# Delta rule: both passes prepared in slots of the gate chunks

## What is computed

```python
r, kr, vr, z_b, w_down, a_down = _split(_token_shift(u_rwkv, mu), RWKV_SIZES)
w = -jax.nn.softplus(-(rwkv_w0 + jnp.tanh(w_down) @ rwkv_w2)) - 0.5
decay = jnp.exp(-jnp.exp(w))                  # exp(-exp(-0.5) * sigmoid(...))
a = jax.nn.sigmoid(rwkv_a0 + a_down @ rwkv_a2)
kk = heads(kr * rwkv_k_k); kk = kk / jnp.maximum(norm(kk), L2_EPS)
kr = kr * (1.0 + (a - 1.0) * rwkv_k_a)
def step(S, inp):                             # over the tokens, the delta rule
    sa = jnp.einsum('bhvk,bhk->bhv', S, -kk_t)
    S = S * w_t + sa * (kk * a)_t + v_t * k_t
    return S, jnp.einsum('bhvk,bhk->bhv', S, r_t)
y = groupnorm(y) * rwkv_ln_w + rwkv_ln_b
bonus = jnp.sum(r * kr * rwkv_r_k, -1) * vr
o_b = (y + bonus) * jax.nn.silu(z_b)
m = sigmoid(g_a) * (o_a @ w_proj_fox) + sigmoid(g_b) * (o_b @ w_proj_rwkv)
return x + m @ w_out
```

## Time and profile before

| | us |
|---|---|
| runs | median 3121.57 of 3 (3117.95 to 3123.22) |
| profiled execution | 3119.44, its span 3117.5 |
| TensorE busy | 2993.9 (96%) |
| DVE busy | 1848.9 (59%) |
| ACT busy | 1371.2 (44%) |
| mean granted clock of TensorE | 0.977 of full |

### The profile page before, as it was taken

The page is one execution under the profiler, slowest core; times in us unless marked ns, Lnnn a source line. Parts: engine busy times, 40 slices in busy tenths (PEclk is TensorE's granted clock), DMA queues, the critical chain, the costliest instruction groups (busy, mean ns, idle before and its releaser), DMA issues.

```text
span 3117.5 us, 45946 instructions
## 1 busy us (share of the span) xinstructions
PE 2993.9 (96%) x17935; PEld 2484.0 (80%) x17935; DVE 1848.9 (59%) x2047; ACT 1371.2 (44%) x1876; POOL 344.8 (11%) x371
## 2 busy tenths in 40 slices
PE   8999999999999987999999999999999999986898
PEld 6888788788888877888888888887888888765786
DVE  5555567856665769455555555556445664467664
ACT  5555454343444454444444344445444444422244
POOL 2000011930001948000000000000000000000000
PEclk9999999999999987999999999999999999988999
DMA  7555476675757984566566665655666678701364
GB/s 242 173 171 165 153 223 200 218 224 168 223 186 240 244 255 120 170 193 211 186 193 189 190 188 189 190 185 168 179 198 192 189 213 255 215 23 46 121 211 155
DMA packets 302691, 580.98 MB, mean 186 GB/s; under 512 B 21512, under 2 KB 40200, under 8 KB 300832
## 3 DMA queue, kind: packets, MB, share of 16 engines
q1 hardware_dynamic: 285696, 522.85, 54.5%
q0 software_dynamic: 9264, 37.29, 4.2%
q10 hardware_dynamic: 7536, 18.06, 1.9%
HBM read 550.35 MB, written 21.50 MB: 183 GB/s over the span
## 4 chain that ended last, share of the span: by engine, by line
PE 90%; DVE 6%; ACT 1%; issue 1%; POOL 1%; DMA 1%; ACTq 0%; SPq 0%; DVEq 0%; POOLq 0%
PE acc L940 26%; PE acc L947 26%; PE acc L941 26%; PE tp L955 2%; DVE wL L2260 2%; PE acc L1568 1%; PE acc L1569 1%; PE acc L1575 1%; PE tp L1481 1%; PE acc L1479 1%; PE wk L1226 0%; POOL xs L883 0%; DVE A L3049 0%; PE acc L1241 0%; DMA raw<-in_a_w_in_dram 0%
## 5 line engine op out<-in xcount | busy, mean ns | idle before, releaser
L2260 DVE TENSOR_TENSOR wL<-raw,wH 128x1024 fp32r<-128x1024 f32 (+1 forms) x968 | 1227.4, 1276 | 1124.8 <-ACT wH L1603 1122.9
L1603 ACT CAST wH<-raw 128x1024 fp32r<-128x1024 f32 (+1 forms) x968 | 1009.6, 1045 | 1416.2 <-PE acc L947 1227.2
L940 PE MATMUL acc<-wH,xH 128*128 128x512 f32 (+1 forms) x2208 | 866.5, 393 | 7.0 <-DVE xL L2314 4.2
L941 PE MATMUL acc<-wH,xL 128*128 128x512 f32 (+1 forms) x2208 | 856.8, 389 | 0.0
L940 PE MATMUL acc<-wH,hH 128*128 128x512 f32 x1536 | 603.5, 393 | 1.9 <-DVE hL L2314 1.9
L941 PE MATMUL acc<-wH,hL 128*128 128x512 f32 x1536 | 600.0, 391 | 0.0
L947 PE MATMUL acc<-wL,xH 128*128 128x512 f32 (+1 forms) x2208 | 588.1, 388 | 1.2 <-DVE wL L2260 1.2
L940 PEld LDWEIGHTS acc<-wH,xH 128*128 128x128 f32 x2208 | 415.9, 188 | 94.9 <-issue 5.0
L947 PEld LDWEIGHTS acc<-wL,xH 128*128 128x128 f32 x2208 | 413.1, 188 | 87.5 <-DVE wL L2260 1.9
L941 PEld LDWEIGHTS acc<-wH,xL 128*128 128x128 f32 x2208 | 416.1, 188 | 82.8
L947 PE MATMUL acc<-wL,hH 128*128 128x512 f32 x1536 | 412.4, 390 | 5.8 <-DVE wL L2260 5.7
(11 more groups left out here) (461 smaller groups left out, 2195.3 us busy)
## 6 DMA issues: line engine op xcount, KB each, us to landing
raw<-in_mlp_w_dram SPq DMA_DIRECT2D x512, 512.0 KB, 3.8
raw<-in_w_in_dram SPq DMA_DIRECT2D x192, 512.0 KB, 3.8
raw<-in_a_w_in_dram SPq DMA_DIRECT2D x96, 512.0 KB, 3.8
raw<-in_b_w_glu_dram SPq DMA_DIRECT2D x64, 512.0 KB, 3.6
raw<-in_a_w_out_dram SPq DMA_DIRECT2D x32, 512.0 KB, 3.7
raw<-in_w_out_dram SPq DMA_DIRECT2D x32, 512.0 KB, 4.5
raw<-in_w_proj_fox_dram SPq DMA_DIRECT2D x16, 512.0 KB, 4.8
raw<-in_w_proj_rwkv_dram SPq DMA_DIRECT2D x16, 512.0 KB, 4.4
```

What stands on the lines that cost most here:

```text
L940: nc.tensor.matmul(bank, aH[:, k, rows], wH[:, j % SPLIT, u, 0:n], start=k == 0, stop=False)
L941: nc.tensor.matmul(bank, aL[:, k, rows], wH[:, j % SPLIT, u, 0:n], start=False, stop=False)
L1603: nc.scalar.copy(wH[:, j % SPLIT, :, 0:n], raw[:, j % RAW, :, 0:n]).then_inc(high_done, 1)
L2260: nc.vector.tensor_tensor(wL[:, j % SPLIT, :, 0:n], raw[:, j % RAW, :, 0:n], wH[:, j % SPLIT, :, 0:n].bitcast(F32), ALU.subtract).then_inc ...
```

## The change

Both passes are prepared inside the slots of the gate chunks. For that each pass has its own buffers, only four banks are used (C[0] to C[3], once the attention's), and the steps are laid out over ten slots per pass: p = 3 + 10 m + s. TensorE makes `lin` at s = 0, `cum` at s = 2, the totals at s = 4, transposes at s = 6 and s = 8. The biases come as a row of weights against a row of ones. The three triangles of the sums become two: they hold ones and are fp32r, the sigmoid is split into a rounded part and a rest (`sgH`, `sgL`), the inclusive sum is the exclusive one plus the sigmoid itself (on DVE), and the factor goes into the scale of the exponential. The vectors are loaded by POOL, three of them one after the other through one buffer, `par`.

On POOL, while the constants are made and after the token shift's loads:

```diff
+    for e, by in enumerate((1, -1)):
+        blocks(decay[:, e], 1.0)
+        keep(decay[:, e], [[by, P]], -1, -by)
...
+    pool.wait_ge(f_dve, FDVE["og", 1])
+    for m in range(MT):
+        for v, (low, bias) in enumerate((("rwkv_w2_2", "rwkv_w0_2"), ("rwkv_a2_2", "rwkv_a0_2"))):
+            pool.dma_start(lw2[m][0:LORA, v], I[low][0]).then_inc(r_low_in[m], 16)
+            pool.dma_start(lw2[m][LORA:LORA + 1, v], I[bias]).then_inc(r_low_in[m], 16)
+        if m == 0:
+            pool.wait_ge(shift_out, 17)
+            bcast("rwkv_k_k_2", par[:], r_par_in)
+    for m in range(MT):
+        if m:
+            pool.wait_ge(r_dve, RDVE["kt", m - 1])
+            bcast("rwkv_k_k_2", par[:], r_par_in)
+        pool.wait_ge(r_dve, RDVE["kk0", m])
+        bcast("rwkv_k_a_2", par[:], r_par_in)
+        pool.wait_ge(r_dve, RDVE["ka", m])
+        pool.dma_start(par[:], I["rwkv_r_k_2"].rearrange("o h n -> o (h n)").broadcast_to([P, H1])).then_inc(r_par_in, 16)
+    pool.wait_ge(r_pe, RPE["L", 0])
+    bcast("rwkv_ln_w_2", lnw[:], r_ln_in)
+    bcast("rwkv_ln_b_2", lnb[:], r_ln_in)
```

On TensorE, the steps (in `prep_lin`, `prep_cum`, `prep_tot`, `prep_turn`), the slots and what waits there:

```diff
+    for v in range(2):
+        for q in range(2):
+            last = nc.tensor.matmul(C[2 * v + q], lT[:, v, m * P:m * P + P], lw2[m][:, v, q * NW:(q + 1) * NW],
+                                    start=True, stop=True)
+    RPE.mark(r_pe, last, "lin", m)
...
+    wait(name_dve=("sgL", m))
+    wait(("siga", m))
+    for e in range(2):
+        for q in range(2):
+            bank = C[2 * e + q]
+            cols = slice(q * NW, (q + 1) * NW)
+            nc.tensor.matmul(bank, decayR[:, e], sgH[m][:, cols], start=True, stop=False)
+            last = nc.tensor.matmul(bank, decayR[:, e], sgL[m][:, cols], start=False, stop=True)
+    RPE.mark(r_pe, last, "cum", m)
...
+    wait(("E3", m))
+    for p in range(R_PAIRS):
...
+    wait(("T", m, 3) if part else ("lam", m))
+    pairs = ((kkh[m][:], "kkh"), (rr[:, m], "rh")) if part else ((E1[m][:], "bh"), (E2[m][:], "kh"))
+    for i, (src, name) in enumerate(pairs):
+        wait(name_dve=(name, m))
...
+    if s == 0:
+        prep_lin(m)
+    if s == 2:
+        prep_cum(m)
+    if s == 4:
+        prep_tot(m)
+    if s in (6, 8):
+        prep_turn(m, s // 2 - 3)
 for k in range(8):
-    product(t.chunk + k, t.fill + k, (k + 1) % 2, xH, xL)
+    product(t.chunk + k, t.fill + k, (k + 1) % 2, xH, xL, between=lambda i: prep_slot(3 * k + i))
+    prep_slot(3 * k + 2)
...
+pe.wait_ge(r_act, RACT["T", 1, 7])
```

The transposes of `fo` come in two halves, one before the scores and one between their second and third part. In the core the scores of the second pass wait for parts of the first, each for the bank that it writes; `Y` stands before the first `S` (its own matmuls are unchanged), and the projection waits for `S` instead of `O`:

```diff
+        if m:
+            if j == 2:
+                wait(("Y", m - 1, 1))
+            wait(name_dve=("O", m - 1, 1) if j == 3 else ("S", m - 1, 1))
+        elif j == 2:
+            turn_half(fo, range(2, 4))
+        elif j == 3:
+            pe.wait_ge(group_free, t.group + 6)
+        b0 = (0, 2, 6, 4)[j]
...
+    RPE.mark(r_pe, last, "Y", m)
...
-pe.wait_ge(r_dve, RDVE["O", 1, 1])
...
+pe.wait_ge(r_dve, RDVE["S", 1, 1])
```

On ACT, with `factor` for E0 and E3, and the gates' load for the mixing before the second pass' end:

```diff
+    nc.scalar.activation(dst[:, halves[0]], C[bank], ACT.Exp, scale=NEG_DECAY)
+    RACT.mark(r_act, nc.scalar.activation(dst[:, halves[1]], C[bank + 1], ACT.Exp, scale=NEG_DECAY), name, m)
...
+    if p == 5:
+        act.wait_ge(shift_out, 17)
+        for i in range(MT):
+            RACT.mark(r_act, nc.scalar.activation(zs[:, i], zb[:, i], ACT.Sigmoid), "sz", i)
+    m, s = (p - 3) // 10, (p - 3) % 10
+    if not 0 <= m < MT:
+        return
+    if s == 1:
+        act.wait_ge(r_dve, RDVE["kks", m])
+        RACT.mark(r_act, nc.scalar.activation(rsm[:, 1], rsm[:, 0], ACT.Sqrt), "sqrt", m)
+        act.wait_ge(r_pe, RPE["lin", m])
+        if m:
+            act.wait_ge(r_dve, RDVE["zz", 1])
+        nc.scalar.activation(sg[m][:, halves[0]], C[0], ACT.Sigmoid)
+        RACT.mark(r_act, nc.scalar.activation(sg[m][:, halves[1]], C[1], ACT.Sigmoid), "sigw", m)
+        act.wait_ge(r_act, RACT["sigw", m])
+        RACT.mark(r_act, nc.scalar.copy(sgH[m][:], sg[m][:]), "sgH", m)
+        nc.scalar.activation(sa[m][:, halves[0]], C[2], ACT.Sigmoid)
+        RACT.mark(r_act, nc.scalar.activation(sa[m][:, halves[1]], C[3], ACT.Sigmoid), "siga", m)
+    if s == 3:
+        act.wait_ge(r_dve, RDVE["sum", m, 1])
+        RACT.mark(r_act, nc.scalar.activation(E2[m][:], E1[m][:], ACT.Exp, scale=-NEG_DECAY), "E2", m)
+        RACT.mark(r_act, nc.scalar.activation(E1[m][:], E1[m][:], ACT.Exp, scale=NEG_DECAY), "E1", m)
+        act.wait_ge(r_dve, RDVE["bon", m])
+        factor("E0", bt[m], 0, m)
+        factor("E3", par, 2, m)
+    if s == 5:
+        act.wait_ge(r_pe, RPE["tot", m])
+        RACT.mark(r_act, nc.scalar.activation(lamT[:, m].rearrange("p a c -> p (a c)"), C[0][:, 0:2 * R_PAIRS], ACT.Exp), "lam", m)
+    if s in (7, 9):
+        if s == 7:
+            act.wait_ge(r_dve, RDVE["bt", m])
+        for i in range(2 * s - 14, 2 * s - 10):
+            dst = (bkT if i < 4 else kkrT)[m][:, 4 * (i % 2):4 * (i % 2) + 4, (i // 2) % 2]
+            act.wait_ge(r_pe, RPE["T", m, i])
+            RACT.mark(r_act, nc.scalar.copy(dst, C[i % 4].rearrange("p (a t) -> p a t", a=4)), "T", m, i)
...
+    if c == 1:
+        act.wait_ge(r_dve, RDVE["yb", 1])
```

On DVE (`keys_scaled` also takes the rest `sgL`; `normed_keys`, `keys_mixed`, `bonus` and `decayed` hold the operations that L3000 to L3038 made, kk0 to kks, kkm to kk, ka to b, bo0 to bon, and kkh, rh, bh), then the end of the first pass behind the levels of the second:

```diff
+    dve.wait_ge(r_act, RACT["sgH", m])
+    step(TT(sgL[m][:], sg[m][:], sgH[m][:].bitcast(F32), ALU.subtract), "sgL", m)
...
+        step(TT(E1[m][:, cols], C[q], sg[m][:, cols], ALU.add), "sum", m, q)
...
+def prep_slot(p):
+    if p == 1:
+        shift_mix(7)
+        step(nc.vector.memset(lT[LORA:LORA + 1], 1.0), "one")
+    if p == 10:
+        for i in range(MT):
+            dve.wait_ge(r_act, RACT["sz", i])
+            step(TT(zb[:, i], zb[:, i], zs[:, i], ALU.mult), "zz", i)
+    m, s = (p - 3) // 10, (p - 3) % 10
+    if not 0 <= m < MT:
+        return
+    if s == 0:
+        normed_keys(m)
+    if s == 1:
+        keys_scaled(m)
+    if s == 2:
+        keys_mixed(m)
+    if s == 3:
+        running(m)
+        bonus(m)
+    if s == 4:
+        decayed(m)
+    if s == 5:
+        own("bh", m)
+        step(TT(E2[m][:], kr[:, m], E2[m][:], ALU.mult), "kh", m)
+    if s == 6:
+        own("kkh", m)
+        step(TT(bt[m][:], sa[m][:], par[:], ALU.mult), "bt", m)
+        step(TT(kr[:, m], kr[:, m], par[:], ALU.mult), "kt", m)
+slot_chunks(prep_slot, lambda k: None)
...
+        if m == 0 and j == 2:
+            low_half(0, range(2, 4))
+            t.high += 4
...
+        if m and lv == 1:
+            end_mean(0)
+        if m and lv == 2:
+            end_centre(0)
+        if m and lv == 3:
+            end_square(0)
+        if m and lv == 4:
+            end_sums(0)
+    if m:
+        end_gated(0)
```

More of the change, by code:

```diff
@@ L195, in rwkv_steps @@
         dve += [("O", m, e) for e in range(2)]
-    end(MT - 1)
+    act += [("sd", 1)]
+    dve += ends[1]
     return pe, act, dve
@@ L1385, in _, with wait, prep_lin @@
             t.fill += 8
+            C = [tp[0], tp[1], wk[0], wk[1]]
+            C = [b[:].rearrange("p a s -> p (a s)") for b in C]
+            B = [acc[0][0], acc[0][1], acc[1][0], acc[1][1]]
+            B = [b[:] for b in B] + C
+            def wait(name_act=None, name_dve=None):
+                if name_act:
+                    pe.wait_ge(r_act, RACT[name_act])
+                if name_dve:
+                    pe.wait_ge(r_dve, RDVE[name_dve])
+            def prep_lin(m):
+                pe.wait_ge(r_low_in[m], 64)
+                wait(name_dve=("one",))
+                if m:
+                    wait(("T", m - 1, 7))
+                else:
+                    pe.wait_ge(f_act, FACT["fv", F_ITEMS - 1])
+                for v in range(2):
[3 more added lines that the diff above has]
+                RPE.mark(r_pe, last, "lin", m)
@@ L1398, in _ @@
+            turn_half(fo, range(2))
             pe.wait_ge(acc_free, 2 * t.fill + 4)
[L1399 to L1405 removed]
             half = [slice(0, TC), slice(TC, P)]
@@ L1454, in _ @@
                     for e, c in quads:
-                        last = nc.tensor.matmul(B[e][half[c], p * TC:(p + 1) * TC], kkrT[half[e], p, 0, half[c]],
-                                                bkT[half[e], p, 0, half[c]], start=True, stop=True)
+                        last = nc.tensor.matmul(B[e][half[c], p * TC:(p + 1) * TC], kkrT[m][half[e], p, 0, half[c]],
+                                                bkT[m][half[e], p, 0, half[c]], start=True, stop=True)
                 RPE.mark(r_pe, last, "L", m)
@@ L2221, in _ @@
             load_gates(0)
+            end(MT - 1)
+            high_half(8)
             g0 = t.group
@@ L3026, in _, with running, bonus @@
-                own("b", m)
+                own("kk", m)
+                step(TT(sa[m][:], kkh[m][:], sa[m][:], ALU.mult), "b", m)
+            def running(m):
+                dve.wait_ge(r_pe, RPE["cum", m])
+                for q in range(2):
+                    cols = slice(q * NW, (q + 1) * NW)
+                    step(TT(E1[m][:, cols], C[q], sg[m][:, cols], ALU.add), "sum", m, q)
+            def bonus(m):
+                own("k'", m)
```

(2 more changed lines are left out.)

449 lines of the change are left out of this document (195 added, 254 removed).

## The result

The changed kernel takes 3081.96 us (median of 4 runs, 3076.6 to 3084.74) beside 3120.19 us of the kernel before (4 runs, 3117.95 to 3123.22): ratio 0.9875, 95% interval 0.9858 to 0.9892, so 38 us less. The profiled execution took 3081.5 us with a span of 3079.8; the prediction said 3081.2 and 3079.3.

A forecast was written before the change was run, and what follows sets the result against it. TensorE was taken to bound the gate chunks and a chain hopping between engines the two preparations. 31.7 − 32.2 − 41.4 + 5.2 − 1.5 = −38.2 us gave a forecast of 3081 us, range 3068 to 3100.

The forecast's parts named there:

- inserts are paid one for one: Gate chunks: TensorE is always busy, so inserted work lengthens them by its own time, 10.4 us a pass, 20.9 for both.
- Changing operand kind: Gate chunks: ten inserts of another operand kind cost 0.2 us extra each, 2 us in all, bounds 0 and 3.5.
- Waits: Gate chunks: TensorE stalls 1.9 us before the first pass' sums, 1.25 and 3.95 before the totals; 7.1, bounds 0 and 13.
- the rival of a drain at every table: ACT's table switches at s = 1 take twice as long, sums' stall 4.5 us, time 3084; chance 0.03.
- Low clock: Gate chunks: the clock falls behind the long stall, eight slow instructions, 1.6 us; 1.7 in all, bounds 0 and 5.
- First preparation: Between last gate matmul and first pass' masks: most of the exposed chain goes, saving 32.2 us, bounds 29 and 34.
- Second preparation: Between first pass' last outputs and second pass' masks: the chain goes, saving 41.4 us, bounds 39 and 42.
- First pass' end between the levels: Normalization on DVE after levels 1 to 4 of the second pass delays them: +5.2 us, bounds 2 and 6.
- The six operations behind level 5: Second pass, DVE: 7.5 us of the first pass' normalization, free since DVE waited 6.80 there and Y adds four more.
- End: After the second core: DVE loses the product with the gate, weight casts no longer wait for issuing gates; −1.5 us.
- the wait for E3: Totals at s = 4 need ACT's E3, ready 9.4 us after the slot before begins: stalls of 1.25 and 3.95 us.
- Broadcasts on POOL and the ring behind ACT's long slot: Gate chunks: vector loads on POOL cost nothing; four weight units cover ACT leaving s = 3 late by 6.7 us.

The follow-up runs named there:

- the three moves: Changed kernel with the totals one slot later, the root behind the sigmoids and the first pass' end pieces in VectorE's idle time: 3064.29 us, ratio 0.9824.
- the second profile: The changed kernel run once more without any edit, beside the experiments on the same chip: 3084.85 us, ratio 0.9892.
- the kernel with the second pass outside: Changed kernel with only the first pass prepared in the slots, the second pass' steps behind the last gate matmul: 3096.5 us, ratio 0.9935.
- Y back: Changed kernel with the matmuls of Y between the two state steps again, as in the kernel before: 3077.80 us, run once.

## Why the prediction was right

The mechanism was that of the sum, in both halves: TensorE pays for the inserts and for the waits at three slots, and the two exposed preparations go. The total was closer than its terms: the gate chunks cost 2.6 us more and the first core 1.7 more than forecast, the gains were 1.2 larger, and 2.7 us ahead of the changed stretch made up for most of the rest.

- **TensorE bounds the gate chunks, and inserts are paid one for one:** shown by the doubled transposes, +7.0 for 6.96, and by the three moves, where nothing but the inserts is left (170.4 + 21.4 = 191.8 against 191.85). Work 21.4 us against 20.9 predicted.
- **Changing operand kind:** mis-sized. I took 2 us, from slots of attention; in the gate chunks sums, fp32 products and transposes cost little beside their own time, 21.4 measured against 20.9 summed, so 0.5 at most for all ten.
- **Waits:** 7.23 against 7.1, each within 0.12 us of its forecast, with the releasers foreseen (the rest of the decays, ScalarE's last exponential). ScalarE's steps behind the first are those of the sum; the rows answer to the earlier trace rows:

```profile
2585.46 1.28 ACT L2203 ACT_TABLE_LOAD   x1
2586.76 0.22 ACT L2203 ACTIVATE rsm<-rsm 128x16 f32<-128x16 f32 x1
2586.99 1.28 ACT L2207 ACT_TABLE_LOAD   x1
2588.29 0.60 ACT L2207 ACTIVATE sg<-tp 128x512 f32<-128x512 f32 x1
```

  Each change of table takes 1.28 us and the load starts within 0.02 of the end of the operation before, so the rival of a drain at every table falls. By the Trainium skill, ScalarE: Activation LUTs, What ACT_TABLE_LOAD costs, a drain of about 1.38 us would be added; these rows do not agree. The prediction priced this rival for the first pass alone; by the same sum the second pass' sums, ready after 7.3 + 2.6 = 9.9 us in slots of 8.16, would have waited 1.7 too, so 3085 and not 3084. In the trace TensorE waits for no sums of the second pass.
- **Low clock:** the term that was mis-sized. 1.7 us forecast; the stops cost 5.6 beyond their length (3.9 in the second profile), of which the clock is about 4.8 (3.1) and the restarts, which the sum left out, the rest. I had taken one stretch of eight slow matmuls from the projection. Behind the wait of 3.97 us it lasts longer, 3.1 to 3.5 us lost in each of ten profiles, and to the short waits I had given next to nothing: that of 1.24 us costs 1.87 in four profiles and 0.2 to 0.3 in seven, that of 2.02 costs 1.9 in two and 0.3 in eight. By that estimate the clock alone stayed within its bound of 5. Together with the operand term the gate chunks came out 2.6 us longer, and the eight chunks at 174.1 + 34.3 = 208.4, just over the 208 I had named.
- **First preparation,** −33.0 against −32.2. The sum had 2731 − 2719.5 = 11.5 us from the end of the last gate matmul; from that end it is 10.7, and the 11.81 of the table count from the start of its group. **Second preparation,** −41.4 as forecast, 6.10 us. That the slots are what gives 32.4 of it is shown by the kernel with the second pass outside.
- **First pass' end between the levels:** +5.0 against +5.2, of which the levels are 1.33 + 3 × 1.13 = 4.7. The six operations behind level 5 hold VectorE for 7.7 us where it had waited 6.0 in the second pass of the kernel before (not the 6.80 of the first, which the prediction took), so kkrT comes 1.6 us later, 11.13 us behind QQ of level 5 instead of 9.57:

```profile
2900.26 1.28 DVE L3077 TENSOR_TENSOR kkrT<-kkrT,tp 128x512 f32<-128x512 f32 x2 [6.01 <-PE tp L1501]
...
2865.51 1.28 DVE L3208 TENSOR_TENSOR kkrT<-kkrT,tp 128x512 f32<-128x512 f32 x2
```

  The first row is of the kernel before, the second of the changed one. Yet TensorE has no wait for kkrT: it comes to the state products only 17.8 us behind that QQ. The way from kkrT to yy is 1.3 us shorter, and from QQ of level 5 to yy it is 22.19 us against 21.94 before. So the six operations are free to within 0.3 us, as the prediction had it. Its second cover, Y ahead of the state products, wasn't needed: with Y back TensorE has no wait for kkrT either.
- **First core,** +1.7 against 0: 1.54 is level 1 at the low clock, which is absent in the second profile. In that one the core is 51.58, and the state steps vary by 0.5. So no cost of the change itself can be told, save perhaps for Y; whether it brings the low clock into level 1 isn't known either, since there is one profile of the kernel before.
- **End,** −1.7 against −1.5, in the two parts that were foreseen: the transposes of zb begin 14.75 us behind yy instead of 15.89 (the product with the gate, 1.23), and the projection's second half 3.68 us behind the last of them instead of 4.28 (the issues of the gates). No run takes the two apart.
- **Slips in the sums,** each of 0.1 us and without weight: twice 10.4 is 20.8 and not 20.9, the terms of the wait for E3 add to 9.3 and not 9.4, those of the end to −1.4 and not −1.5.
- **Broadcasts on POOL and the ring behind ACT's long slot** cost nothing, as foreseen: the three vectors landed after 5.2 to 5.5 us, VectorE waited for none of them, and TensorE has no wait in the gate chunks other than those three.

```profile
PE tp L1444 <- ACT par L2188: 5.2, 2, 4.0
PE tp L1436 <- DVE sgL L3037: 2.0, 1, 2.0
```

  These are all of TensorE's waits in 2541 to 2741, and none follows up to the last gate matmul; the kernel before had none in its gate chunks.

What the totals lost, and with it the largest avoidable loss of the change, was in the prediction as a price and not as a question: it put 5.2 us of waits and the clock on a step that nothing needed before the next slot.

## What to carry to other kernels

When a chain of small steps moves into the slots of a stage that one engine bounds, its price is that engine's own time for the inserts and the waits at slots too close together, with what follows each wait: work out for each step when its input is ready, and put the consumer a slot later where nothing is in a hurry for it. A wait on TensorE may cost about its own length once more, as the clock falls behind it (up to 1.9 us behind waits of 1.24 and 2.02, 3.1 to 3.5 behind one of 3.97). Work for an idle engine belongs behind its last operation before a wait, not behind the one that others wait for: the same 1.2 us cost 1.13 in one place and nothing four operations earlier.

## What was not expected of the hardware

- The clock falls behind an idle time of 3.97 us every time, and behind one of 1.24 or 2.02 us only in some executions of the same program; in level 1 of the first pass' inverse it fell in 9 of 14 profiles, always for 1.54 us (7.48 instead of 5.94). What decides is open: no run takes it apart.
- A stop at the full clock costs 0.2 to 0.3 us beyond its length all the same.
- Whether the matmuls behind the idle time are small or of full width makes little difference: 3.5 and 3.1 us lost.
- Eight fp32 matmuls of two columns (sixteen records) take 1.84 us, as much as eight fp32r ones of 512 columns (1.82).
